# Value pages loaded by one engine, and sums of squares of two norms made by TensorE and GpSimd, in a hybrid decoder step

## The reference

```
proj = rmsnorm(x) @ w_in                       # q, k, v, gate z, SSD inputs
attn = rmsnorm(attend(q, k, v), g_attn)        # 16 heads; samples attend to 256 cached positions
y    = ssd(...) * silu(z)                      # SSD group, width 1024
y    = _rms(y in 2 groups of 512) * g_ssd      # _rms: x * rsqrt(mean(x*x) + 1e-6)
out  = concatenate([attn, y]) @ w_out          # (264 x 2048) @ (2048 x 1024)
```

## Time and profile before

| what | value |
|---|---|
| median of three runs | 1185.89 us |
| the profiled execution | 1185.12 us |
| its span | 1182.9 us |
| PE busy | 1145.5 us (97%) |
| DVE busy | 793.8 us (67%) |
| ACT busy | 568.4 us (48%) |
| POOL busy | 752.0 us (64%) |
| chain that ended last, by engine | PE 71%, all others 1% or less |

### The profile page before, as it was taken

One profiled execution on the slowest core, in us unless ns is written; L12 is line 12 of the kernel. 1 busy time (PEld: TensorE's weight loads), 2 busy tenths in 40 slices (PEclk: granted clock), 3 DMA queues, 4 the chain that ended last, 5 costly groups with the idle time before them and its releaser, 6 DMA issues.

```text
span 1182.9 us, 24246 instructions
## 1 busy us (share of the span) xinstructions
PE 1145.5 (97%) x7585; PEld 1011.8 (86%) x7585; DVE 793.8 (67%) x1727; ACT 568.4 (48%) x1286; POOL 752.0 (64%) x633
## 2 busy tenths in 40 slices
PE   9999999769999999999999999999999999999997
PEld 7877777538889999999999999998888888888876
DVE  6689796883289998000899999993544556765534
ACT  3323223543344655565555554444555555555545
POOL 0066350144545898988666666666776798789654
PEclk9999999888999999999999999999999999999999
DMA  7568666783544566666455554444666698788653
GB/s 255 163 221 279 188 211 212 270 289 89 179 153 133 160 189 188 186 179 194 136 142 143 143 143 143 143 142 146 188 189 190 187 316 268 232 279 291 192 153 108
DMA packets 108411, 225.13 MB, mean 190 GB/s; under 512 B 12754, under 2 KB 21570, under 8 KB 107818
## 3 DMA queue, kind: packets, MB, share of 16 engines
q1 hardware_dynamic: 104130, 209.45, 57.3%
q0 software_dynamic: 3264, 11.54, 2.8%
q10 hardware_dynamic: 936, 3.14, 0.7%
HBM read 215.80 MB, written 8.19 MB: 189 GB/s over the span
## 4 chain that ended last, share of the span: by engine, by line
PE 71%; issue 1%; DVE 0%; POOL 0%; ACT 0%; DVEq 0%; POOLq 0%; ACTq 0%
PE bank L1681 31%; PE bank L1711 30%; PE bank L1691 5%; PE bank L1634 2%; PE bank L1646 1%; PE bank L1658 1%; PE bank L1731 0%; PE bank L1748 0%; POOL hl L1574 0%; DVE acts L2107 0%; PE bank L1739 0%; ACT acts L1917 0%; POOL hl L1559 0%; PE bank L1766 0%; PE bank L1724 0%
## 5 line engine op out<-in xcount | busy, mean ns | idle before, releaser
L1559 POOL TENSOR_TENSOR hl<-ring,hl 128x512 fp32r<-128x512 f32 x448 | 585.9, 1317 | 184.9 <-ACT hl L1797 177.3
L1797 ACT CAST hl<-ring 128x512 fp32r<-128x512 f32 x512 | 317.1, 620 | 289.8 <-PE bank L1711 159.6
L1681 PE MATMUL bank<-split,hl 128*128 128x256 f32 x3072 | 378.4, 282 | 0.4 <-ACT hl L1797 0.3
L1681 PEld LDWEIGHTS bank<-split,hl 128*128 128x128 f32 x3072 | 366.2, 188 | 0.8 <-issue 0.5
L1711 PE MATMUL bank<-hl,split 128*128 128x512 f32 x1524 | 353.6, 394 | 0.0
L1711 PEld LDWEIGHTS bank<-hl,split 128*128 128x128 f32 x1524 | 286.0, 188 | 67.7 <-issue 0.9
L522 PE MATMUL pj<-xn,ring 128*128 128x264 f32 x672 | 158.4, 391 | 0.7 <-ACT proj L803 0.7
L2077 DVE TENSOR_TENSOR split<-acts,split 128x256 fp32r<-128x256 f32 x128 | 130.4, 1043 | 37.8 <-ACT split L1893 34.2
L522 PEld LDWEIGHTS pj<-xn,ring 128*128 128x128 f32 x672 | 126.1, 192 | 24.9 <-issue 4.6
L2084 DVE TENSOR_TENSOR hl<-ring,hl 128x512 fp32r<-128x512 f32 x64 | 46.7, 730 | 116.7 <-ACT hl L1797 116.7
L2043 DVE TENSOR_SCALAR bv<-bkey,ig 128x130 f32<-128x130 f32 x256 | 86.0, 395 | 0.0
(11 more groups left out here) (369 smaller groups left out, 1133.3 us busy)
## 6 DMA issues: line engine op xcount, KB each, us to landing
ring<-in_uv SPq DMA_DIRECT2D x256, 256.0 KB, 2.7
ring<-in_v_rows SPq DMA_DIRECT2D x256, 256.0 KB, 3.1
ring<-in_w_ring SPq DMA_DIRECT2D x76, 512.0 KB, 4.2
room<-in_cache_k SPq DMA_DIRECT2D x64, 128.0 KB, 2.6
hs<-in_state_ssm SPq DMA_DIRECT2D x8, 512.0 KB, 5.4
out_ssm_s<-hs SPq DMA_DIRECT2D x8, 512.0 KB, 5.9
acts<-x_rows SPq DMA_DIRECT2D x8, 512.0 KB, 4.2
room<-in_cache_v SPq DMA_DIRECT2D x12, 256.0 KB, 3.1
```

What stands on the lines that cost most here:

```text
L1559: nc.gpsimd.tensor_tensor(hl[:, r % HL, 1], raw[:, r], hl[:, r % HL, 0].bitcast(F32), ALU.subtract).then_inc(lo_done, 1)
L1681: mm = nc.tensor.matmul(out, hl[:, r % HL, m, k * P:(k + 1) * P], split[:, x, kk, 0:TP], start=(kk == 0 and n == 0), stop=(kk == KD - 1 an ...
L1797: nc.scalar.copy(hl[:, r % HL, 0], raw[:, r]).then_inc(hi_done, 1)
```

## The change

Four edits, all in the mixer:

1. SP issues all value units, in the order 0 to 7. POOL issues none.
2. The squares of the two SSD groups are no longer added by DVE. PE sums four chunks each by four matmuls with the ones, into `yb` and `pj[1]`, before the value units. Both groups get one reciprocal and one root, over 528 columns. ACT squares both groups ahead of the exponentials of block 7, and makes the first two casts of weights right behind the sums.
3. The squares of the attention output, chunks 0 to 6, are made and added by POOL as the chunks come, and chunk 7 by ACT; PE sums two chunks. This sum now stands ahead of the first half.
4. Order: value unit 4 moves behind the first half, and 5, 6 and 7 each behind one half more or less; the transposes of block 7 move behind units 0 and 1; ACT casts pieces 8 and 9 ahead of the samples' squares; DVE copies the samples' own scores ahead of `masked(7)`.

```diff
@@ -283,6 +283,7 @@
+sum_bank = [yb, pj[1]]
@@ -377,7 +378,7 @@
-sp.wait_ge(unit_used, {0: KU - 2, 5: KU + 1, 7: KU + 4}[n])
+sp.wait_ge(unit_used, {0: KU - 2, 3: KU - 1, 4: KU, 5: KU + 1, 6: KU + 3, 7: KU + 4}[n])
@@ -435,12 +436,13 @@
-values(2)
+for n in range(2, 5):
+    values(n)
-values(5)
-values(7)
+for n in range(5, VU):
+    values(n)
@@ -483,23 +485,17 @@
-def values(n):
-    q, m, g = n // (2 * NPG), n // NPG % 2, n % NPG
-    pool.wait_ge(unit_used, {3: KU - 1, 4: KU, 6: KU + 3}[n])
-    for j in range(SIDE):
-        b = q * SIDE + j
-        at = pool.value_load(ptab[0:1, b * NPG + g:b * NPG + g + 1], min_val=0, max_val=t["n_pool"] - 1)
-        pool.dma_start(val_homes[V_HOME[n]][:, j],
-                       t["cache_v"][bass.ds(at, 1)].rearrange("a p n -> p (a n)")[:, m * 4 * P:(m + 1) * 4 * P]
-                       ).then_inc(val_full[n], 16)
-pool.wait_ge(ptab_in, 16)
-values(3)
-values(4)
+pool.wait_ge(st_done, KD)
+for c in range(KD - 1):
+    pool.wait_ge(o_copied, 2 * c + 2)
+    to = sq_att[:, c and 1 + c % 2, 0:TP]
+    nc.gpsimd.tensor_tensor(to, mix[:, c, 0:TP], mix[:, c, 0:TP], ALU.mult).then_inc(sq_c, 1)
+    if c:
+        pool.wait_ge(sq_c, c + 1)
+        if c >= 2:
+            pool.wait_ge(pre_p, c - 1)
+        nc.gpsimd.tensor_tensor(sq_att[:, 0, 0:TP], sq_att[:, 0, 0:TP], to, ALU.add).then_inc(pre_p, 1)
-    if n == 2:
-        values(6)
@@ -699,20 +695,21 @@
                               start=(c == 0), stop=(c == KD - 1))
 mm.then_inc(own_ready, 1)
 turn_sample_probs()
-pe.wait_ge(pre_s, 1)
+pe.wait_ge(y_done, KD)
 pe.wait_ge(own_copied, 1)
-nc.tensor.matmul(pj[1][:, 0:NT], ones, sq0[:, 0], start=True, stop=True).then_inc(sum_s, 1)
-turn_probs(KD - 1)
+for n in range(GROUPS):
+    pe.wait_ge(sq_s, n + 1)
+    for k in range(4):
+        of = sq1[:, k] if n else sq0[:, k] if k < 3 else mix[:, KD - 1]
+        mm = nc.tensor.matmul(sum_bank[n][:, 0:NT], ones, of, start=(k == 0), stop=(k == 3))
+    mm.then_inc(sum_s, 1)
 pe.wait_ge(h1_done, KD)
 value_unit(0)
 value_unit(1)
+turn_probs(KD - 1)
 attend(KD - 1)
 value_unit(2)
-pe.wait_ge(pre_s, 2)
-nc.tensor.matmul(pj[0][:, 0:NT], ones, sq1[:, 0], start=True, stop=True).then_inc(sum_s, 1)
 value_unit(3)
-pe.wait_ge(y_done, KD)
-value_unit(4)
 def out_half(i, d, half, start, stop):
@@ -755,17 +752,20 @@
 pe.wait_ge(pj_copied, N_IN)
 pe.wait_ge(sums_read, 2)
+pe.wait_ge(o_copied, 2 * KD)
+pe.wait_ge(pre_p, KD - 2)
+pe.wait_ge(sq_p, 1)
+nc.tensor.matmul(hd[0][:, 0:TP], ones, sq_att[:, 0, 0:TP], start=True, stop=False)
+nc.tensor.matmul(hd[0][:, 0:TP], ones, sq_att[:, KD - 1, 0:TP], start=False, stop=True).then_inc(sum_p, 1)
 out_half(N_IN, 0, 1, True, False)
+value_unit(4)
+out_half(N_IN + 1, 1, 1, True, False)
 value_unit(5)
-pe.wait_ge(o_copied, 2 * KD)
-pe.wait_ge(pre_p, 1)
-nc.tensor.matmul(hd[0][:, 0:TP], ones, sq_att[:, 0, 0:TP], start=True, stop=True).then_inc(sum_p, 1)
-out_half(N_IN + 1, 1, 1, True, False)
-value_unit(6)
 values(0)
 out_half(N_IN + 2, 2, 1, True, False)
+value_unit(6)
+out_half(N_IN + 3, 3, 1, True, False)
 value_unit(7)
-out_half(N_IN + 3, 3, 1, True, False)
 values(1)
 spread_rates()
 out_half(N_IN + 4, 4, 1, True, False)
@@ -914,7 +914,6 @@
-act.wait_ge(pre_s, 1)
@@ -942,25 +941,6 @@
-gates(0)
-gates(1)
-for b in range(NQ):
-    sample_exps(b)
-exps(KD - 1)
-squares(0)
-squares(1)
-probs_out(KD - 1)
-act.wait_ge(diffs6, 2)
-nc.scalar.activation(s6[:, 4:6], s6[:, 4:6], ACT.Exp, scale=SCALE).then_inc(rates6, 1)
-attended(KD - 1)
-act.wait_ge(var_s, 1)
-nc.scalar.activation(tmp[:, 0], tmp[:, 0], ACT.Sqrt).then_inc(root_s, 1)
-act.wait_ge(o_copied, 2 * KD)
-act.wait_ge(ys_done, KD)
-nc.scalar.activation(sq_att[:, :, 0:TP], mix[:, 0:KD, 0:TP], ACT.Square).then_inc(sq_p, 1)
-act.wait_ge(var_s, 2)
-nc.scalar.activation(tmp[:, 1], tmp[:, 1], ACT.Sqrt).then_inc(root_s, 1)
@@ -970,7 +950,25 @@
             act.wait_ge(o_used, n - HL + 1)
         nc.scalar.copy(wo[:, n % HL, 0], raw_o[:, n % RAW]).then_inc(o_hi, 1)
+gates(0)
+gates(1)
+for b in range(NQ):
+    sample_exps(b)
+squares(0)
+squares(1)
+exps(KD - 1)
+act.wait_ge(sum_s, 2)
 out_high(0, 2)
+probs_out(KD - 1)
+act.wait_ge(diffs6, 2)
+nc.scalar.activation(s6[:, 4:6], s6[:, 4:6], ACT.Exp, scale=SCALE).then_inc(rates6, 1)
+act.wait_ge(var_s, 1)
+nc.scalar.activation(tmp[:], tmp[:], ACT.Sqrt).then_inc(root_s, 1)
+attended(KD - 1)
+act.wait_ge(o_copied, 2 * KD)
+act.wait_ge(ys_done, KD)
+nc.scalar.activation(sq_att[:, KD - 1, 0:TP], mix[:, KD - 1, 0:TP], ACT.Square).then_inc(sq_p, 1)
 for n in range(2):
     act.wait_ge(mixed_s, 4 * n + 4)
     nc.scalar.copy(mixr[:, KD + 4 * n:KD + 4 * n + 4], mix[:, KD + 4 * n:KD + 4 * n + 4]).then_inc(mix_hi, 1)
@@ -981,9 +979,10 @@
+out_high(8, 10)
-out_high(8, 11)
+out_high(10, 11)
@@ -1255,9 +1254,9 @@
+        dve.wait_ge(own_ready, 1)
+        nc.vector.tensor_copy(s6[:, 3], pj[1][:, OWN:OWN + NQ]).then_inc(own_copied, 1)
-dve.wait_ge(own_ready, 1)
-nc.vector.tensor_copy(s6[:, 3], pj[1][:, OWN:OWN + NQ]).then_inc(own_copied, 1)
@@ -1271,10 +1270,6 @@
-dve.wait_ge(sq_s, 1)
-link(nc.vector.tensor_tensor(sq0[:, 0], sq0[:, 0], sq0[:, 1], ALU.add),
-     nc.vector.tensor_tensor(sq0[:, 2], sq0[:, 2], mix[:, KD - 1], ALU.add))
-nc.vector.tensor_tensor(sq0[:, 0], sq0[:, 0], sq0[:, 2], ALU.add).then_inc(pre_s, 1)
@@ -1289,26 +1284,19 @@
-def ssd_factor(n):
-    dve.wait_ge(sum_s, n + 1)
-    nc.vector.tensor_scalar(tmp[:, n], pj[1 - n][:, 0:NT], GROUPS / D, EPS, ALU.mult, ALU.add).then_inc(sums_read, 1)
-    dve.wait_ge(sums_read, n + 1)
-    nc.vector.reciprocal(tmp[:, n], tmp[:, n]).then_inc(var_s, 1)
-    dve.wait_ge(root_s, n + 1)
+    dve.wait_ge(root_s, 1)
-ssd_factor(0)
-dve.wait_ge(sq_s, 2)
-link(nc.vector.tensor_tensor(sq1[:, 0:2], sq1[:, 0:2], sq1[:, 2:4], ALU.add))
-nc.vector.tensor_tensor(sq1[:, 0], sq1[:, 0], sq1[:, 1], ALU.add).then_inc(pre_s, 1)
-ssd_factor(1)
+for n in range(GROUPS):
+    dve.wait_ge(sum_s, n + 1)
+    nc.vector.tensor_scalar(tmp[:, n], sum_bank[n][:, 0:NT], GROUPS / D, EPS, ALU.mult, ALU.add).then_inc(sums_read, 1)
+dve.wait_ge(sums_read, GROUPS)
+nc.vector.reciprocal(tmp[:], tmp[:]).then_inc(var_s, 1)
@@ -1331,10 +1319,6 @@
-dve.wait_ge(sq_p, 1)
-for n in (4, 2):
-    link(nc.vector.tensor_tensor(sq_att[:, 0:n, 0:TP], sq_att[:, 0:n, 0:TP], sq_att[:, n:2 * n, 0:TP], ALU.add))
-nc.vector.tensor_tensor(sq_att[:, 0, 0:TP], sq_att[:, 0, 0:TP], sq_att[:, 1, 0:TP], ALU.add).then_inc(pre_p, 1)
```

More of the change, by code:

```diff
@@ L318, in build @@
              "pt6_ready", "pts_ready", "cleared6", "diffs6", "rates6", "fe_ready", "spread6", "v6_ready", "v6_masked", "att_s"))
-        pre_s, pre_p, pre_l, pre1, xg_done, early_out = map(sem, ("pre_s", "pre_p", "pre_l", "pre1", "xg_done", "early_out"))
+        sq_c, pre_p, pre_l, pre1, xg_done, early_out = map(sem, ("sq_c", "pre_p", "pre_l", "pre1", "xg_done", "early_out"))
         sums_read, o_hi, o_lo, o_used, mix_hi, mix_lo = map(sem, (
```

## The result

The changed kernel takes 1178.34 us (median of 10 runs, 1173.5 to 1182.7) against 1186.36 us (10 runs, 1184.18 to 1188.18) for the kernel before on the same chip: ratio 0.993, 95% interval 0.9912 to 0.9948. It was timed again on three further occasions, beside the experiments: 1174.9, 1176.79 and 1177.55 us, against 1186.62, 1186.5 and 1186.66 of before. Over all 26 runs the median is 1177.3. The forecast was 1175, range 1170.5 to 1182, faster.

The account below looks back on a forecast made before the run. PE was taken to bound the kernel, waiting four times on norms of the mixer's output. Gains of 7.2 and 3.7 us, less 0.2, took the profiled 1185.12 to 1174.4; plus 0.77 made 1175, range 1170.5 to 1182.

Parts of the forecast that it names:

- first term: From the samples' exponentials to the first output-projection half: it starts at 245.1 in place of 252.29, 7.2 us gained.
- Squares to reciprocal: SSD norm chain: squares from 228.4, eight matmuls ending at 235.8, one reciprocal of 3.6 us, one root of 0.65.
- table load: ACT's load before the root: carries no wait and lies under DVE's reciprocal, so no time counted.
- Scaling: DVE scales eight SSD tiles while POOL is idle: 3.3 us, against 5.25 beside POOL.
- contention rival: DVE's scaling runs beside POOL (+2.0) and POOL's burst of squares costs 3.6: gain 5.2, 1180.7 us; chance 0.14.
- First half: Start of the output projection's first half: at 245.1 us in place of 252.29, 7.2 gained.
- First half's clock: First half at 2.4 GHz, since the gap ahead is less than half of 7.06: 1.9 us gained.
- clock rival: Clock falls before the first half (5.1 us), sums at 1.2 GHz to their end (+1.2): gain 7.8, 1178; chance 0.10.
- Second term: From the first half to the second set of halves: 32.0 us in place of 35.7, 3.7 gained.
- wait before the samples' values: New PE wait behind unit 7 for DVE's two maskings, which a half hid before: 1.4 us lost.
- Ring: Weight-ring reload starts at 252.7, first tile lands by 264.3 at worst; margin 3 to 4 us before the fifth half, costed at nothing.
- POOL's squares: POOL's 13 squares and additions, nine in a burst from 175.8: 0.2 us of PE, bounds 0 and 3.6.

Follow-up runs that it names:

- e1: The changed kernel timed again without any edit, second occasion: median 1174.9 us (4 runs), 0.9903 of before.
- e2: Changed kernel with the stores of keys, values and state moved behind the first four weight-ring reloads on SP: 1175.35 us, 0.9913 of before.
- e10: e9 plus 4 unread matmuls ahead of the transposed probabilities and 4 ahead of the first half: 1170.73 us, 0.9866 of before.
- e9: Changed kernel with three moves: unit 7 ahead of the fourth half, selection behind units 5 to 7, stores behind four ring reloads: 1177.18 us.
- e12: The changed kernel timed again without any edit, fourth occasion: median 1177.55 us (6 runs), 0.993 of before.
- e6: Changed kernel with unread matmuls in PE's three gaps and the output stores behind the first four ring reloads: 1173.76 us, 0.9897 of before.
- e11: Changed kernel with 4 unread matmuls only in the gap before the first half: 1174.83 us, 0.9913 of before.
- e4: Changed kernel with value units 3, 4 and 6 issued by POOL again, all else as changed: 1178.97 us, 0.9939 of before.

## Why the prediction was right

The forecast time (1175) is 2.3 us under the pooled median of 1177.3 and 3.3 under the first, inside the range, and the sign is right with the interval clear of 1. The mechanism is right too: the norms' two big waits went or shrank (5.45 to none, 7.06 to 2.24), and the stage gave 10.88 us in the trace for the 10.9 worked out. That the two agree to 0.1 is luck: the first term came 0.76 over and the second 0.78 under, and the four traces of the changed kernel give 10.88, 11.26, 10.87 and 10.32. By its own steps:

- **Squares to reciprocal.** Squares 227.66 (forecast 228.4, and this trace is 0.64 ahead). The eight matmuls took 4.8 us (228.98 to 233.8; forecast 6.2). The prediction let the clock fall just ahead of them and come back 5.1 us after them; in this trace it was low from 227.8, so already for the transposes (1.12 for 0.66), to 231.1, only 2.1 us into the sums. In e1, where it didn't fall there, the first half came 1.06 earlier for it. The prediction's reading of the earlier trace rows, that PE had had only the transposes since the projection when the clock fell, is also wrong: between the last projection tile and 226.77 PE ran small matmuls without a gap. Reciprocal 3.45 (3.6), root 0.64 (0.65).
- **The table load** was costed at nothing "under the reciprocal". It stands behind other work of ACT and ended 0.66 us after the reciprocal. ACT's last square was late too, so the attention sum waited 0.53 where no wait was forecast; the first half waits for DVE behind it in any case.
- **Scaling** 3.32 (3.3), with POOL idle. POOL in the changed kernel, the rows on either side of it (239.14 to 242.4), the second beginning after a gap of 7.09:

```profile
234.57 2.51 POOL L500 TENSOR_TENSOR wo<-ring,wo 128x512 fp32r<-128x512 f32 x2 [13.80 <-ACT wo L951]
244.17 4.31 POOL L500 TENSOR_TENSOR wo<-ring,wo 128x512 fp32r<-128x512 f32 x3 [7.09 <-ACT wo L951]
...
251.85 2.80 POOL L500 TENSOR_TENSOR wo<-ring,wo 128x512 fp32r<-128x512 f32 x2 [1.36 <-ACT wo L951]
```

 Beside POOL (251.85 to 254.65) the same operation on the attention takes 5.29, although its tiles are smaller (L1330 at 250.82). The contention rival is out at the first place. The Trainium skill (SBUF — State Buffer, SBUF: two separate sides) has the rule that a VectorE operation with two SBUF inputs and a GpSimd operation block one another; these two rows agree with it in kind.
- **First half** 18.23 after the anchor, forecast 19.0, so 7.96 gained for 7.2. Errors of 1.4 (sums), 0.7 (table load) and small ones cancelled in part.
- **First half's clock.** "I let PE keep its clock: -1.9" was wrong in most traces: 4.7 where 3.25 was forecast, so 0.4 was won here and not 1.9. The clock rival had this with a chance of 0.10, and its 1178 is nearer to the first occasion's 1178.34 than the forecast's 1175. Its other half, sums at 1.2 GHz to their end, came in none of the four traces.
- **Second term** 2.92 for 3.7. The loss at the first half (1.5) is partly made up at the fifth (4.68 for 5.20). The wait before the samples' values came as forecast (1.41 for 1.4), in all four traces of the changed kernel.
- **Ring.** Loaded from 256.68, not 252.7 (the 0.8 us of SP between units was counted at nothing), and cast at 265.99, not by 264.3 at worst. In the four traces of the changed kernel the cast began 1.1 to 2.9 us ahead of the half, not 3 to 4. It held, and e2 shows it costs nothing.
- **POOL's squares.** They ran at 174.93 to 181.7, and PE waited 0.32 at 182.97 (0.2 forecast; a wait between 176 and 205 was named as a sign of being wrong, and this is a small one). The contention rival was right here for DVE: beside the squares L1197 took 0.84 for 0.42 and a pair of L1150 1.50 for 0.61, and from L1194 (174.86) to the end of L1162 DVE took 8.4 us for 4.9. Its wait of 2.94 behind this in before took up most of the difference. Timelines of the changed kernel, first and last rows of POOL's burst, then PE:

```profile
174.93 1.37 POOL L492 TENSOR_TENSOR bcb<-mix 128x256 f32<-128x256 f32 x2
...
180.87 0.86 POOL L497 TENSOR_TENSOR bcb<-bcb 128x256 f32<-128x256 f32 x1
```
```profile
182.97 0.41 PE L543 MATMUL hd<-cst,proj 128*128 128x128 f32 x2 [0.32 <-DVE proj L1199]
```

- **The mis-sized term is the clock outside the counted waits.** The sum took the profiled execution's time at 1.2 GHz as a fixed part of the program and shifted its result by 0.77 to a median. It isn't fixed in the changed kernel: over the 26 runs of it the span rises by 0.46 us for each us of low clock (correlation 0.91), from an intercept of 1165.6. The profiled execution had 14 us at the low clock (0.994) and the first occasion 22.8 on the mean: 4.0 of the 4.8 us between that execution and the median. On all four occasions the profiled execution was the fastest or second fastest of its runs, so the trace shows the changed kernel at its best. That the clock is the cause and not a sign of it is what e10 against e9 shows: work that only keeps PE occupied took 12.9 us of low clock and 6.5 us of time away.

Open: at which places the slower executions lose the clock. Each trace is of one execution, and those of the changed kernel have 0.993 or more; they show the five places, but not which of them have more in a run of 0.986, nor why e12 keeps the clock over the same wait of 2.24. Open too is what the second edit (the SSD sums) and the fourth (the order) are worth apart, since neither was taken back alone. Not all spread is clock either: one run of e6 took 1178.06 at 0.994 and one of e11 1178.64 at 0.993, unprofiled, cause unknown.

## What to carry over

Where several engines work to let PE go on, count a chain by its own steps from one anchor just ahead of it; the sum of this one came out right, though single steps missed by 1.5 and cancelled. Give the clock a term of its own with a spread, since a profile shows one execution and a median has others. And when waits have become short, try the cheapest thing first: eight unread matmuls in two gaps of 1.7 and 2.2 us brought 6.5 us on top of the three moves, nearly as much as the whole change.

## Of the hardware, not expected

- The granted clock fell to 0.51 with PE busy all 3.00 us, at 16 records of 128x16 behind 16 of 128x4 (e10); the 16 records of 128x16 took 1.94 to 3.49 in different executions.
- With POOL issuing eight pages at the same time, the pages of unit 2 landed 9.5 us after issue in place of 4.8, and held PE for 3.86 us in e4 and not at all in the changed kernel.
- SP left about 0.8 us between the last page of one value unit and the first of the next, though the home was free.
- The granted clock of one unchanged program varied from 0.986 to 0.995 between executions, and its time from 1173.5 to 1182.7.
